# Adding the two expert rows of each token at the end of a diffusion-transformer step: whole tiles per transfer, and three of five adds on GpSimd

## The reference

```python
def _rmsnorm(x, g):
    xf = x.astype(jnp.float32)
    y = xf * lax.rsqrt(jnp.mean(xf * xf, axis=-1, keepdims=True) + EPS)
    return (y * g.astype(jnp.float32)).astype(x.dtype)

    # in _layer: g2 * (sum of the two chosen experts' outputs, weighted)
    x = x + g2[:, None] * _moe(h2, P, l)
    # in reference
y_prompt = _rmsnorm(xp, norm_final)      # 128 context tokens
y_sample = _rmsnorm(xs, norm_final)      # 512 latent tokens
```

## Time and profile before

| | us |
|---|---|
| median of 3 runs (lowest, highest) | 1138.26 (1137.2, 1140.0) |
| the profiled execution | 1139.36 |
| its span | 1137.70 |
| PE busy in the span | 1029.0 (90%) |
| DVE busy | 531.5 (47%) |
| ACT busy | 221.6 (19%) |
| POOL busy | 212.9 (19%) |

### The profile page before, as it was taken

The page is one execution under the profiler, slowest core; times in us unless marked ns, Lnnn a source line. Parts: engine busy times, 40 slices in busy tenths (PEclk is TensorE's granted clock), DMA queues, the critical chain, the costliest instruction groups (busy, mean ns, idle before and its releaser), DMA issues.

```text
span 1137.7 us, 13951 instructions
## 1 busy us (share of the span) xinstructions
PE 1029.0 (90%) x5151; PEld 621.5 (55%) x5151; DVE 531.5 (47%) x1256; ACT 221.6 (19%) x425; POOL 212.9 (19%) x282
## 2 busy tenths in 40 slices
PE   4999999999999999999999899999867999969670
PEld 2566766876465555655666566645544555535330
DVE  4655766043658446446478424145633323222226
ACT  4110001000234343443411100021210111101002
POOL 3140000010492000111111141112211232322210
PEclk9999999999999999999999999999968999989895
DMA  9921220251442332223223561301499999999957
GB/s 317 372 78 64 74 74 1 63 159 31 135 132 78 112 111 67 83 93 116 88 75 111 188 191 37 129 38 75 158 398 391 397 408 409 406 406 407 405 227 277
DMA packets 101283, 209.94 MB, mean 185 GB/s; under 512 B 8968, under 2 KB 64710, under 8 KB 101088
## 3 DMA queue, kind: packets, MB, share of 16 engines
q1 hardware_dynamic: 87984, 179.19, 43.3%
q0 software_dynamic: 13136, 29.82, 7.6%
q10 hardware_dynamic: 96, 0.04, 0.0%
HBM read 197.93 MB, written 18.83 MB: 191 GB/s over the span
## 4 chain that ended last, share of the span: by engine, by line
PE 81%; DMA 8%; DVE 5%; issue 3%; SPq 2%; POOL 0%; ACT 0%; DVEq 0%; POOLq 0%
PE pair L1913 20%; PE pair L1906 16%; PE pair L2257 6%; PE pair L1942 6%; PE pair L1909 4%; PE pair L1905 4%; DMA dft_region<-in_w_e_up 4%; PE pair L2274 4%; PE pair L2063 3%; PE pair L2149 3%; PE pair L2286 2%; PE pair L2040 2%; DMA hyena_region<-in_w_e_up 2%; PE pair L2003 1%; PE pair L2096 1%
## 5 line engine op out<-in xcount | busy, mean ns | idle before, releaser
L1906 PE MATMUL pair<-hT_region,ring_region 128*128 128x512 f32 x352 | 181.6, 598 | 0.0
L1905 PEld LDWEIGHTS pair<-hT_region,ring_region 128*128 128x128 f32 x352 | 65.5, 191 | 77.3 <-issue 75.6
L893 POOL TENSOR_TENSOR dft_region<-dft_region,padded_region 128x640 f32<-128x640 f32 x24 | 37.0, 1543 | 322.8 <-DVE padded_region L1494 322.8
L1838 DVE TENSOR_TENSOR mixer_region<-pair,mixer_region 128x128 f32<-128x128 f32 x34 | 9.9, 291 | 143.0 <-ACT mixer_region L1160 143.0
L1913 PE MATMUL pair<-hT_region,ring_region 128*128 128x320 f32 x256 | 75.3, 449 | 0.3 <-DMA ring_region<-in_w_gate 0.3
L2257 PE MATMUL pair<-ring_region,padded_region 128*64 128x256 f32 x640 | 73.5, 382 | 1.3 <-DMA ring_region<-in_w_e_up 1.3
L1942 PE MATMUL pair<-ring_region,dft_region 128*128 128x512 f32 x160 | 71.4, 596 | 0.5 <-issue 0.3
L1905 PE MATMUL pair<-hT_region,ring_region 128*128 128x128 f32 x352 | 69.5, 279 | 1.8 <-DVE hT_region L1610 1.5
L916 POOL DMA_INDIRECT moe_pairs<-padded_region,bias_region x34 | 34.4, 1012 | 189.2 <-DVE padded_region L1852 172.6
L1494 DVE TENSOR_TENSOR padded_region<-pair,padded_region 128x640 f32<-128x640 f32 x24 | 19.8, 825 | 103.5 <-PE pair L1906 69.4
L1913 PEld LDWEIGHTS pair<-hT_region,ring_region 128*128 128x128 f32 x256 | 50.0, 197 | 23.1 <-issue 4.6
(11 more groups left out here) (411 smaller groups left out, 1796.8 us busy)
## 6 DMA issues: line engine op xcount, KB each, us to landing
ring_region<-in_w_ada SPq DMA_DIRECT2D x24, 1024.0 KB, 7.8
ring_region<-in_w_gate SPq DMA_DIRECT2D x16, 1024.0 KB, 5.8
ring_region<-in_w_in SPq DMA_DIRECT2D x13, 1024.0 KB, 5.6
ring_region<-in_w_e_gate SPq DMA_DIRECT2D x12, 1024.0 KB, 12.8
ring_region<-in_w_e_up SPq DMA_DIRECT2D x12, 1024.0 KB, 18.8
ring_region<-in_w_e_down SPq DMA_DIRECT2D x24, 512.0 KB, 16.8
hT_region<-in_w_e_gate SPq DMA_DIRECT2D x7, 1024.0 KB, 12.8
hT_region<-in_w_e_up SPq DMA_DIRECT2D x7, 1024.0 KB, 18.3
```

What stands on the lines that cost most here:

```text
L893: pool.tensor_tensor(merged[:, dj, :], merged[:, dj, :], gtmp, ALU.add).then_inc(merged_add, 1)
L1905: mm(ps_[0:m, W0:W0 + TC], lhsT, rhs[:, 0:TC], start=start, stop=stop)
L1906: return mm(ps_[0:m, W0 + TC:1024], lhsT, rhs[:, TC:T], start=start, stop=stop)
```

## The change

The ten reads become six. Tiles 1 to 4 are each read by one transfer of 1 MB, with both rows of each token. Tile 0 is read in two transfers of 512 KB, the first with columns 0 to 511 of both rows, the second with the others, each with a semaphore of its own, and VectorE adds each half by itself (two adds of 128x512 in place of one of 128x1024). For tiles 2, 3 and 4 (`ADDED` = 2 and up) a = a + b is done by GpSimd, which waits for `fin_in[t]` and raises `pairs_added`; VectorE waits for that before x1 = x1 + a. VectorE's list is reordered: the norm of tile 1 stands ahead of the add of tile 2. The sums are the same, and the writes of the results are too.

```diff
+        ADDED = 2
+        first_in, pairs_added = [sem(f"first_rows_in{h}") for h in range(2)], sem("pair_rows_added")
...
             sp.wait_ge(scatters_done, 1)
-            for t in range(NT):
-                for s in range(2):
-                    sp.dma_start(fin_d[t][:, s, :], out_d[s * T + t * P:s * T + (t + 1) * P, :]
-                                 ).then_inc(fin_in[t], 16)
+            both_rows = out_d.rearrange("(s t p) d -> t p s d", s=2, p=P)
+            for h in range(2):
+                half = slice(HD2 * h, HD2 * (h + 1))
+                sp.dma_start(fin_d[0][:, :, half], both_rows[0][:, :, half]).then_inc(first_in[h], 16)
+            for t in range(1, NT):
+                sp.dma_start(fin_d[t], both_rows[t]).then_inc(fin_in[t], 16)
...
             pool.sem_inc(scatters_done, 1)
+
+            for t in range(ADDED, NT):
+                pool.wait_ge(fin_in[t], 16)
+                pool.tensor_tensor(fin_d[t][:, 0, :], fin_d[t][:, 0, :], fin_d[t][:, 1, :], ALU.add).then_inc(pairs_added, 1)
...
             dve.wait_ge(nfin_in, 16)
-            for n in range(NT + 1):
-                if n < NT:
-                    a, b = fin_d[n][:, 0, :], fin_d[n][:, 1, :]
-                    dve.wait_ge(fin_in[n], 32)
+            def with_pairs(n):
+                a, b = fin_d[n][:, 0, :], fin_d[n][:, 1, :]
+                if n == 0:
+                    for h in range(2):
+                        half = slice(HD2 * h, HD2 * (h + 1))
+                        dve.wait_ge(first_in[h], 16)
+                        tt(a[:, half], a[:, half], b[:, half], ALU.add).then_inc(fin_sum, 1)
+                elif n < ADDED:
+                    dve.wait_ge(fin_in[n], 16)
                     tt(a, a, b, ALU.add).then_inc(fin_sum, 1)
-                    dve.wait_ge(fin_sum, n + 1)
-                    tt(x1[:, n, :], x1[:, n, :], a, ALU.add).then_inc(fin_sq, 1)
-                if n:
-                    t = n - 1
-                    dve.wait_ge(fin_rms, t + 1)
-                    link(dve.reciprocal(rstd[:, t:t + 1], rms[:, t:t + 1]))
-                    stt(x1[:, t, :], x1[:, t, :], rstd[:, t:t + 1], fin_n, ALU.mult, ALU.mult).then_inc(fin_done, 1)
+                if n < ADDED:
+                    dve.wait_ge(fin_sum, n + 2)
+                else:
+                    dve.wait_ge(pairs_added, n - ADDED + 1)
+                tt(x1[:, n, :], x1[:, n, :], a, ALU.add).then_inc(fin_sq, 1)
+
+            def last_norm(t):
+                dve.wait_ge(fin_rms, t + 1)
+                link(dve.reciprocal(rstd[:, t:t + 1], rms[:, t:t + 1]))
+                stt(x1[:, t, :], x1[:, t, :], rstd[:, t:t + 1], fin_n, ALU.mult, ALU.mult).then_inc(fin_done, 1)
+
+            for n in range(NT):
+                if n == ADDED:
+                    last_norm(n - 1)
+                with_pairs(n)
+                if n and n != ADDED:
+                    last_norm(n - 1)
+            last_norm(NT - 1)
```

## The result

| | before | changed |
|---|---|---|
| median of 13 runs each (lowest, highest), us | 1138.03 (1137.14, 1140.00) | 1141.45 (1139.95, 1144.83) |
| ratio of times, 95% interval | | 1.0030 (1.0022 to 1.0039) |
| the profiled execution, its span, us | 1139.36, 1137.70 | 1140.84, 1139.2 |
| first issue of the reads, us from the span's start | 1109.57 | 1108.35 |
| from there to tile 1's pair add | 8.23 | 8.02 |

The changed kernel is 3.4 us slower (2.5 to 4.4 by the interval). The two profiled spans differ by only 1.5 us, but in the changed kernel's profiled execution everything ahead of the reads happened to be 1.2 us quicker.

What follows compares the result with a forecast made beforehand. Bound by tile 1's landing, then VectorE's list: 14.46 - 3.75 + 3 x 2.0 = 16.71 us, +2.25, so 1141.6 for the profiled execution and 1140.5 for the median, which stands 1.1 lower; range over the cases 1135.9 to 1142.4.

Steps and rivals of the forecast that it cites:

- What bounds the kernel: At the kernel's end, from 1109 us on: first the landing of tile 1 (1117.80), then VectorE's own list until 1134.67.
- Reads: 0: Reads of the expert rows: six transfers instead of ten change the landing of tile 1 by 0.
- the bounds of -1.0 and +0.9: Limits for tile 1's landing with one transfer for two rows: 1.0 us earlier to 0.9 us later.
- The rival of a landing up to 1.0 us earlier: Exclusion as forecast, but fewer transfers land tile 1 up to 1.0 us earlier: +1.25, so 1139.5 us; chance 0.10.
- Tile 0 in halves: 0: Tile 0's adds on VectorE: x1 ready some 0.6 us earlier, but VectorE then waits longer for tile 1; value 0.
- Three GpSimd adds at 2.0 us each in VectorE's list: Tiles 2 to 4: GpSimd and VectorE exclude each other, so each GpSimd add is inserted into VectorE's list at 2.0 us.
- At most 0.2 us of waiting for ScalarE: Norm of tile 1 moved ahead on VectorE: adds at most 0.2 us of waiting for ScalarE's root.
- the prediction's walk: Expected order at the end, GpSimd adds alternating with VectorE's product 0 and norm 1, then VectorE alone; no landing late.
- The sum: From the first reciprocal to the last product: 14.46 - 3.75 + 3 x 2.0 = 16.71 us, +2.25.
- the rival in which VectorE wins the port: VectorE goes first whenever both want the port, so three GpSimd adds stand exposed: +3.45, so 1141.7 us; chance 0.22.
- No exclusion: GpSimd's adds run beside VectorE, whose last add to x1 starts earlier: -2.7, so 1135.6 us; chance 0.15.

Runs made afterwards that it cites:

- reads-only run: Kernel before with only the change's six reads, all adds on VectorE in the old order: 1138.30 us against 1138.67, ratio 0.9996.
- the copies: Kernel before plus three extra GpSimd copies of 1024 columns, each with one input in SBUF, results unread: ratio 1.0019.
- the fills: Kernel before plus three extra GpSimd fills of 2048 columns that write SBUF and read nothing: 1138.42 us against 1138.67, ratio 0.9999.
- one-add run: Changed kernel with ADDED at 4, so GpSimd adds only the last tile: ratio 1.0016 to the kernel before.
- adds-only run: Changed kernel with the ten reads of before and one whole add for tile 0: 1142.85 us against 1138.67, ratio 1.0036.

## Why the prediction was right, point by point

- **What bounds the kernel.** Landing of tile 1, then VectorE's list: right. In the reads-only run tile 1's add came 0.3 us earlier and the end with it, with 16.88 us between them as before.
- **Reads: 0.** Measured -0.21 us at tile 1's add in the changed kernel, -0.31 in the reads-only run, inside the bounds of -1.0 and +0.9; as a time not to be told from 0, and less than the scatter of kernels with the same ten reads (7.63 to 8.58). The rival of a landing up to 1.0 us earlier has at most about a third of that to show in these two. (The two rows stand in the other order than their caption: `in_w_gate`, 5.8 us, is read in pieces of 1 KB and `in_w_out`, 4.9, in pieces of 4 KB. The prediction uses them rightly.) The advice of the Trainium skill (DMA: Bandwidth & Descriptors, section on bandwidth) to batch to 1 MiB has no visible worth for transfers that queue behind each other here: 0.9996 (0.9987 to 1.0005).
- **Tile 0 in halves: 0.** The value was right, the 0.6 us of earliness named with it was not there. VectorE could begin on the second half only 5.49 us after the first issue (1113.84), where both whole rows had taken 4.90, so x1 of tile 0 was summed no sooner. The eight kernels with this edit have 5.2 to 5.5, the five with ten reads 4.8 to 5.0; the cover of VectorE's wait for tile 1 took it up, and 0.57 us of that wait were left.
- **Three GpSimd adds at 2.0 us each in VectorE's list.** Measured 2.16, 1.89 and 2.13, mean 2.06, so 6.18 in place of 6.0. GpSimd's first add was recorded from 1118.97 on, 0.01 us after the product's recorded start, and went first; a hundredth is too little to say which of the two came up earlier. This agrees with the rule of the Trainium skill (SBUF — State Buffer, section on SBUF's two separate sides) that the two share a port pair which one holds for a whole instruction; the copies, which stop VectorE, and the fills, which don't, fit its words on a GpSimd operation that reads SBUF. Its full 2.34 for each would have been +3.3, the rows' 2.06 gives +2.4.
- **At most 0.2 us of waiting for ScalarE.** Too little: the norm of tile 1 was covered, but the prediction's walk left out that the norm of tile 2, with a single add as its cover, would wait, 0.41 us. The one-add run shows the larger form of the same omission.
- **The sum.** +2.25 was forecast; the trace has -0.2 (reads) + 2.4 (adds) + 0.4 (ScalarE) + 0.1 = +2.7. The ratio's interval, 2.5 to 4.4 us, begins just above the forecast. The time was inside the range, and the direction and the mechanism were right. The time by itself would not have picked this case: 1141.45 lies nearer to the 1141.7 of the rival in which VectorE wins the port than to the 1140.5 of the forecast, and it is the stretched rows that decide between the two. Whether the 0.7 us between trace and medians is real stays open; the adds-only run has the same sign (3.1 traced, 4.1 by its ratio, interval 2.5 to 5.7).
- **VectorE wins the port (+3.45).** Its sign in the profile, idle time of VectorE ended by POOL with no row stretched, is absent. **No exclusion (-2.7):** no row supports it. The prediction gave it 0.15, since met operations were few, and counted four places in the trace of before. There are more: the short GpSimd adds of line 809 meet VectorE's operations of line 1562, whose median is 0.48 us, and seven of those are stretched, as here (the first row merges five adds):

```profile
316.90 2.56 POOL L809 TENSOR_TENSOR hyena_region<-hyena_region 128x256 f32<-128x256 f32 x5
317.05 1.64 DVE L1562 SCALAR_TENSOR_TENSOR hyena_region<-ring_region,scT,hyena_region 128x256 f32<-128x256 f32 x1
```

## What to carry to other kernels

Work moved to another engine is only gone from the first if they don't share what the operation needs. Before GpSimd is given an elementwise operation beside VectorE, look in the trace for places where the two already meet, and read off how long VectorE's row is there against its median; the price of a moved add was 2.06 us in VectorE's list against 1.25 for doing it there. An operation that can read one of its tensors from PSUM was not stopped in any row here. And when an order is changed near the end, walk the list for what covers each wait for another engine: 0.4 us lay in that in the changed kernel, 1.4 in the one-add run.

## What the hardware showed that was not expected

- A GpSimd operation that reads SBUF stops a VectorE operation with two SBUF inputs until 0.13 to 0.21 us ahead of its own recorded end; a fill by GpSimd of 1.80 us does not stop it at all (1.22 to 1.28 us beside it). A VectorE operation with one of its two tensors in PSUM is not stopped by the adds either (0.35 us inside an add of 1.54).
- GpSimd's add of 1024 float32 columns takes 2.34 us with two different tensors and 1.89 us with the same tensor as both inputs; a copy takes 1.04.
- A GpSimd operation that comes up while VectorE works goes ahead of VectorE's next operation, even where VectorE's follow without a gap: in all 13 meetings in the changed kernel and four of the experiments an operation of VectorE was stretched. GpSimd does not always go first, though. In the changed kernel its third add stood ready when the second ended, VectorE's waiting product went ahead of it, and the add took 3.32 us instead of 2.34. In the kernel before, in the rows at 317 us above, VectorE's operation waited through more than one short add in a row. What decides there isn't shown.
- A float32 product of 128x128 by 128x512 is two matmul instructions, 0.43 us from one to the next, while each is shown as 0.59 us long.
